# Expert results of 14 experts summed early by VectorE, those of the last two and of overflow added as one-hot products in PSUM

## The reference, cut to what matters

```python
# per token h: the two chosen experts eid and weights w of a router
gates = (one_hot(eid, 16) * w[..., None]).sum(1)
for e in range(16):
    y = (silu(h @ w_gate[e]) * (h @ w_up[e])) @ w_down[e]      # 1024 -> 512 -> 1024
    out = out + gates[:, e:e + 1] * y
xl = layer_norm(ALPHA * xl + g2_l * out, ln_ffn_g, ln_ffn_b)    # context tiles likewise in layer 0
```

## Time and profile before

| | |
|---|---|
| Time, three runs | 2450.93 us median (2446.91 to 2451.93) |
| The profiled execution | 2452.3 us; its span from the first to the last instruction is 2450.5 us |
| TensorE busy | 2274.0 us (93%), VectorE 1617.8 (66%), ScalarE 1329.9 (54%), GpSimd 242.4 (10%) |
| Mean granted TensorE clock | 0.978 of full speed |
| DMA | 575.35 MB, mean 235 GB/s |

### The profile page before, as it was taken

How to read it: one execution, slowest core, us unless ns; L and a number is a source line. 1 busy time by engine, 2 the same in 40 slices (tenths; PEclk the granted TensorE clock), 3 DMA queues, 4 the chain that set the end, 5 groups by cost and what they waited for, 6 DMA issues and landing times. The chain is left out here.

```text
span 2450.5 us, 29262 instructions
## 1 busy us (share of the span) xinstructions
PE 2274.0 (93%) x11460; PEld 1817.9 (74%) x11460; DVE 1617.8 (66%) x2358; ACT 1329.9 (54%) x2027; POOL 242.4 (10%) x214
## 2 busy tenths in 40 slices
PE   8999999999999999999989998999968997999994
PEld 7887767888788776888876576777756855788872
DVE  5556455655655645665555777899887467899983
ACT  5555544655555545455535614777753352688860
POOL 0001000000000100000003710011114000111101
PEclk9999999999999999999999998999989998999997
DMA  7765585576576567568631038999983334799994
GB/s 274 257 223 181 206 301 172 183 246 228 201 263 218 191 221 277 172 207 308 233 119 37 4 144 306 369 370 354 362 310 112 126 134 172 275 363 366 358 363 186
DMA packets 177731, 575.35 MB, mean 235 GB/s; under 512 B 20133, under 2 KB 28773, under 8 KB 145840
## 3 DMA queue, kind: packets, MB, share of 16 engines
q1 hardware_dynamic: 153120, 504.02, 58.0%
q10 hardware_dynamic: 13808, 51.06, 5.3%
q0 software_dynamic: 10656, 18.29, 2.2%
HBM read 538.69 MB, written 55.15 MB: 242 GB/s over the span
## 5 line engine op out<-in xcount | busy, mean ns | idle before, releaser
L325 DVE TENSOR_TENSOR LO<-RAW,HI 128x1024 fp32r<-128x1024 f32 x558 | 660.0, 1223 | 222.4 <-ACT HI L311 221.2
L311 ACT ACTIVATE HI<-RAW 128x1024 fp32r<-128x1024 f32 x558 | 571.3, 1056 | 371.0 <-PE PS L385 194.3
L383 PE MATMUL PS<-HI,FR 128*128 128x512 f32 (+1 forms) x1776 | 687.3, 387 | 13.6 <-DVE FR L458 7.5
L385 PE MATMUL PS<-HI,FR 128*128 128x512 f32 (+1 forms) x1776 | 680.3, 383 | 0.0
L384 PE MATMUL PS<-LO,FR 128*128 128x512 f32 (+1 forms) x1776 | 679.7, 383 | 0.0
L311 ACT ACTIVATE HI<-RAW,SM 128x512 fp32r<-128x512 f32 (+2 forms) x576 | 361.7, 684 | 276.3 <-PE PS L385 149.4
L327 DVE SCALAR_TENSOR_TENSOR LO<-RAW,SM,HI 128x512 fp32r<-128x512 f32 (+2 forms) x576 | 378.8, 710 | 172.7 <-ACT HI L311 172.5
L383 PEld LDWEIGHTS PS<-HI,FR 128*128 128x128 f32 x1776 | 335.5, 189 | 82.3 <-DVE FR L458 8.7
L385 PEld LDWEIGHTS PS<-HI,FR 128*128 128x128 f32 x1776 | 335.1, 189 | 65.9
L384 PEld LDWEIGHTS PS<-LO,FR 128*128 128x128 f32 x1776 | 335.3, 189 | 62.4
L458 DVE TENSOR_TENSOR FR<-PS,FR 128x512 fp32r<-128x512 f32 x224 | 143.9, 676 | 134.7 <-ACT FR L454 134.1
(11 more groups left out here) (346 smaller groups left out, 2334.6 us busy)
## 6 DMA issues: line engine op xcount, KB each, us to landing
RAW<-in_w_ffn_in SPq DMA_DIRECT2D x88, 1024.0 KB
RAW<-in_w_gate SPq DMA_DIRECT2D x68, 1024.0 KB, 8.5
RAW<-in_w_up SPq DMA_DIRECT2D x68, 1024.0 KB, 10.8
RAW<-in_w_down SPq DMA_DIRECT2D x64, 1024.0 KB
RAW<-in_w_ada SPq DMA_DIRECT2D x48, 1024.0 KB
RAW<-in_w_ffn_out SPq DMA_DIRECT2D x44, 1024.0 KB
RAW<-in_w_in SPq DMA_DIRECT2D x44, 1024.0 KB
YD<-CN ACTq DMA_DIRECT2D x32, 1024.0 KB, 5.4
```

Source lines behind the costliest of these rows:

```text
L311: e.activation(HI[:, i % NSPLIT, c], raw_of(j)[:, c], ACT.Copy, scale=1.0 if g is None else g).then_inc(*hi_done.up())
L325: e.tensor_tensor(LO[:, i % NSPLIT, c], raw_of(j)[:, c], hi, ALU.subtract).then_inc(*lo_done.up())
L383: e.matmul(o, h, hi[:, j, :], start=first and k + j == 0, stop=False)
L385: x = e.matmul(o, ll, hi[:, j, :], start=False, stop=end)
```

## The change

The stage's end is taken apart for the two image tiles. The context tiles keep their old way.

- **Early part.** `dve_late_weights` (expert 2) sets the weight and the slot of a result to zero where its expert is 14 or 15 or an overflow tile. `pool_take` gathers the two rows of each image token when experts 0 to 13 are in `YD`, ahead of `pool_further`. ScalarE scales, VectorE adds, multiplies with the gate and adds `ALPHA` times the stream, 1024 columns at a time, in `XL`.
- **Late part.** `dve_hot` (experts 3 to 6, three instructions of 128x128 each) builds a matrix that has a token's weight at the row that its result has in expert 14 or 15; TensorE transposes four of them in expert 7. The results of 14 and 15 are multiplied with the gate from `x_y` or PSUM (`dve_gate_late`), and `pe_add_late` multiplies them with the matrices into PSUM banks 4 to 7, one per tile and half. Overflow tiles add to the same banks (`more`, `dve_hot_more`) and no longer go through `YD` in layer 1. `dve_add_late` adds the bank to the stream and takes statistics.
- **Norms.** The steps of the attention stage's norm go from the stage's end into the experts: layer 0 one in each of experts 8 to 15, layer 1 one in each of 7 to 10. The six fold steps stand two by two in experts 4 to 6.
- **Tiles.** In layer 0 tile 0 is finished and its input for the attention made while tile 1 is added; the low parts of `qb p0` are placed between. In layer 0 the first two late products stand inside the down product of expert 15.
- **Loads.** Layer 1's last gain and bias (two rows of 4 KB spread over 128 partitions) are loaded after the last expert's weights instead of during the attention. The nine spins are gone.

The core of the diff (left out are the moved buffers, the exact form of `strips` and the counters):

```diff
+def pe_add_late(e, q, l, n, t, h, start, last):
+    q.wait_ge(*dve.at(f"m{l} gated {LATE[n]}{h}"))
+    return e.matmul(PS[4 + 2 * t + h][:, :], x_hot[:, 256 * n + P * t:256 * n + P * t + P],
+                    half_of(x_gated[l][n], h), start=start, stop=last)
...
+    def late(last):
+        if l == 0:
+            for t, h in each:
+                if t:
+                    if h == 0:
+                        for g in range(2):
+                            pe_free(q, 6 + g)
+                    pe_add_late(e, q, l, 0, t, h, True, False)
+                x = pe_add_late(e, q, l, 1, t, h, False, last)
+                if last:
+                    x.then_inc(pe.handle, 1)
+        else:
+            for t, h in each:
+                x = pe_add_late(e, q, l, 1, t, h, False, last)
+                if last:
+                    x.then_inc(pe.handle, 1)
+        return x
+    def more(i, last):
+        q.wait_ge(*more_dve.at(f"m{l} more {i} gated"))
+        for t, h in each:
+            if l == 0:
+                hot, y = x_hot_more[:, P * t:P * t + P], half_of(x_g[1], h)
+            else:
+                hot = x_hot[64 * h:64 * h + 64, 256 * (i % 2) + P * t:256 * (i % 2) + P * t + P]
+                y = x_y[0][64 * h:64 * h + 64, 0:512]
+            x = e.matmul(PS[4 + 2 * t + h][:, :], hot, y, start=False, stop=last)
...
+    def close(i):
+        if i == 0:
+            late(True)
+        elif l:
+            more(i - 1, True)
...
+        if i == 7:
+            q.wait_ge(*dve.at(f"{s} hot"))
+            b = pe_turn(e, q, f"{s} hot T", blocks(x_hot_T), rot)
+            freed[b] = [(act, f"{s} hot in")]
...
+            if i == NE - 1:
+                rot = Banks([0, 1, 2, 3])
...
+            def between():
+                if i == NE - 1:
+                    weighed_T(NE - 1)
+                elif i == NE and l == 0:
+                    q.wait_ge(*act.at(f"{s} hot in"))
+                    for h in range(2):
+                        pe_free(q, 4 + h)
+                        pe_add_late(e, q, l, 0, 0, h, True, False)
...
+    if l == 1:
+        q.wait_ge(*act.at(f"{s} hot in"))
+        for t in range(2):
+            for h in range(2):
+                pe_free(q, 4 + 2 * t + h)
+                pe_add_late(e, q, l, 0, t, h, True, False).then_inc(*pe.up(f"{s} late {t}{h}"))
     pe_further(e, q, l)
...
+        if i == 7:
+            q.wait_ge(*pe.at(f"{s} hot T"))
+            e.activation(x_hot, PS[bank[f"{s} hot T"]][:, :], ACT.Copy).then_inc(*act.up(f"{s} hot in"))
...
+            if i == NE:
+                for t in range(2):
+                    act_add_early(e, q, l, t)
+            for h in range(0 if l and i - 1 in LATE else 2):
                 q.wait_ge(*pe.at(f"{s} y {i - 1}{h} 0"))
+                if i == NE:
+                    q.wait_ge(*dve.at(f"{s} gated {i - 1}{h}"))
...
+            if l == 0 and i > NE - 2:
+                q.wait_ge(*act.at(f"{s} y in {i - 1}1"))
                 e.dma_start(YD[(i - 1) * P:i * P, :], y).then_inc(
...
+def act_add_early(e, q, l, t):
+    y = x_early[l][t][0]
+    q.wait_ge(*dve.at(f"m{l} early weights"))
+    q.wait_ge(*yf_in[t].at(f"m{l} y {t}"))
+    e.activation(y, y, ACT.Copy, scale=x_ew[:, t:t + 1]).then_inc(*act.up(f"m{l} first {t}"))
+def dve_sum_early(e, q, l, t):
+    ya, yb = x_early[l][t]
+    q.wait_ge(*act.at(f"m{l} first {t}"))
+    q.wait_ge(*yg_in[t].at(f"m{l} y {t}"))
+    e.scalar_tensor_tensor(ya, yb, x_ew[:, 2 + t:3 + t], ya, ALU.mult, ALU.add).then_inc(*dve.up(f"m{l} summed {t}"))
+def dve_gate_early(e, q, l, t):
...
+    for h in range(2):
+        q.wait_ge(*g2_in[0].at(f"{s} gate 0"))
+        if l:
+            q.wait_ge(*dve.at(f"{s} summed {n}"))
+        if l == 0 and n == 0:
+            q.wait_ge(*act.at(f"{s} y in {LATE[n]}{h}"))
+        else:
+            q.wait_ge(*pe.at(f"{s} y {LATE[n]}{h} 0"))
+        y = half_of(x_y[n], h) if l == 0 and n == 0 else PS[bank[f"{s} y {LATE[n]}{h}"]][:, :]
+        e.tensor_tensor(half_of(x_gated[l][n], h), y, half_of(HBS[0], h),
...
+def dve_add_late(e, q, l, t, h):
+    s, xs = f"m{l}", half_of(XL[:, t, :], h)
+    q.wait_ge(*pe.at(f"{s} sum {t}{h}"))
+    q.wait_ge(*dve.at(f"{s} z {t}"))
+    e.tensor_tensor(xs, xs, PS[4 + 2 * t + h][:, :], ALU.add).then_inc(*dve.up(f"{s} added {t}{h}"))
+    q.wait_ge(*dve.last())
+    e.bn_stats(stat[:, 16 * t + 6 * h:16 * t + 6 * h + 6], xs).then_inc(*dve.up())
...
 def pool_take(e, q, l, t):
     s, side = f"m{l}", slots(l)
     for k in range(2):
-        if t > 1:
-            q.wait_ge(*dve.at(f"{s} added {t - 2}1"))
-        e.indirect_dma_start(out=x_pair[t % 2][k], out_offset=None, in_=YD[0:X_TILES[l] * NE * P, :],
+        e.indirect_dma_start(out=(x_pair[t % 2] if t > 1 else x_early[l][t])[k], out_offset=None,
+                             in_=YD[0:(X_TILES[l] if t > 1 else 1) * NE * P, :],
                              in_offset=bass.IndirectOffsetOnAxis(ap=side[:, k, t:t + 1], axis=0)).then_inc(
                                  *(yg_in if k else yf_in)[t % 2].up(f"{s} y {t}", by=16))
...
+    e.tensor_scalar(early, col, NE - 2.5, None, ALU.is_lt).then_inc(*dve.up())
+    for n, late in enumerate(LATE):
+        e.tensor_scalar(by_result(x_lw[n]), col, float(late), None, ALU.is_equal).then_inc(*dve.up())
+    q.wait_ge(*dve.last())
+    e.tensor_tensor(slots(l)[:, :, 0:2], slot, early, ALU.mult).then_inc(*dve.up(f"{s} slots"))
+    for n in range(2):
+        e.tensor_tensor(by_result(x_lw[n]), by_result(x_lw[n]), ww, ALU.mult).then_inc(*dve.up())
+    e.tensor_tensor(early, early, ww, ALU.mult).then_inc(*dve.up(f"{s} early weights"))
...
+def dve_hot(e, q, l, n, t):
+    s, row = f"m{l}", by_result(x_gs[:, 0:8])
+    hot, share = x_hot_T[:, 256 * n + P * t:256 * n + P * t + P], by_result(x_lw[n])
+    q.wait_ge(*dve.last())
+    e.tensor_scalar(hot, C["iota"], row[:, 0, t:t + 1], share[:, 0, t:t + 1], ALU.is_equal, ALU.mult).then_inc(*dve.up())
+    e.tensor_scalar(x_hot_tmp, C["iota"], row[:, 1, t:t + 1], share[:, 1, t:t + 1], ALU.is_equal,
+                    ALU.mult).then_inc(*dve.up())
+    q.wait_ge(*dve.last())
+    e.tensor_tensor(hot, hot, x_hot_tmp, ALU.add).then_inc(*dve.up(f"{s} hot" if n and t else None))
...
+        if i == 2:
+            dve_late_weights(e, q, l)
+        if 3 <= i < 7:
+            dve_hot(e, q, l, (i - 3) // 2, (i - 3) % 2)
         if l == 0 and i == 4:
             q.wait_ge(*mod_out[0].at("mod 10"))
-        if l == 0 and 4 <= i < 10:
-            dve_fold_step(e, q, s, (i - 4) // 3, (i - 4) % 3, *x_fold[(i - 4) // 3], x_fold_t)
+        if l == 0 and 4 <= i < 7:
+            for k in (2 * i - 8, 2 * i - 7):
+                dve_fold_step(e, q, s, k // 3, k % 3, *x_fold[k // 3], x_fold_t)
+        if l == 0 and 8 <= i < NE:
+            dve_norm_step(e, q, "o0", "o0 again", (i - 8) // 2, i % 2)
+        if l == 1 and 7 <= i < 11:
+            dve_norm_step(e, q, "o1", "o1", (i - 7) // 2, (i - 7) % 2)
+        if l == 1 and i == 11:
+            dve_hot_more(e, q, l, 0, dve)
...
-    dve_norms(e, q, f"o{l}", ("o0 again", "o1")[l], O_TILES[l])
-    dve_further(e, q, l)
     if l == 0:
+        dve_gate_late(e, q, 0, 0)
+        dve_sum_early(e, q, 0, 0)
+        dve_gate_early(e, q, 0, 0)
+        dve_gate_late(e, q, 0, 1)
+        dve_add_early(e, q, 0, 0)
+        dve_further(e, q, 0)
+        for h in range(2):
+            dve_add_late(e, q, 0, 0, h)
+        dve_stats(e, q, s, 0)
+        dve_sum_early(e, q, 0, 1)
+        q.wait_ge(*pe.at("m0 sum 11"))
+        dve_modulate_b(e, q, 0)
+        dve_gate_early(e, q, 0, 1)
+        lo_parts(e, q, of["qb p0"][0], 1)
+        dve_hidden_lo(e, q, "qb", 0)
+        dve_add_early(e, q, 0, 1)
+        for h in range(2):
+            dve_add_late(e, q, 0, 1, h)
+        dve_stats(e, q, s, 1)
+        lo_parts(e, q, of["qb p0"][0], 1)
+        dve_modulate_b(e, q, 1)
         lo_parts(e, q, of["qb p0"][0])
-        dve_add_up(e, q, 0, 0)
-        dve_add_results(e, q, 0, 1)
-        dve_modulate_b(e, q, 0)
-        dve_add_gated(e, q, 0, 1, 0)
-        dve_hidden_lo(e, q, "qb", 0)
-        dve_add_gated(e, q, 0, 1, 1)
-        dve_stats(e, q, "m0", 1)
-        dve_modulate_b(e, q, 1)
         dve_hidden_lo(e, q, "qb", 1)
     else:
         for t in range(2):
-            dve_add_up(e, q, l, t)
-    if l == 1:
+            dve_sum_early(e, q, 1, t)
+            dve_gate_late(e, q, 1, t)
+        for t in range(2):
+            dve_gate_early(e, q, 1, t)
+            dve_add_early(e, q, 1, t)
+        dve_further(e, q, 1)
+        for t in range(2):
+            for h in range(2):
+                dve_add_late(e, q, 1, t, h)
+            dve_stats(e, q, s, t)
         dve_norms(e, q, s, s, (0, 1))
...
-    q.wait_ge(*more_yd.at(f"{s} all"))
+    for i in (12, 13):
+        q.wait_ge(*yd_out[i % 2].at(f"{s} y {i}"))
     q.wait_ge(*dve.at(f"{s} slots"))
+    if l == 0:
+        q.wait_ge(*pe.at("m0 xT 151"))
```

(25 more changed lines are left out.)

238 lines of the change are left out of this document (160 added, 78 removed).

## The result

The changed kernel takes 2469.91 us in the median (2463.75 to 2472.72, 9 runs), the kernel before 2450.93 us (9 runs). The ratio is 1.0070, 95% interval 1.0056 to 1.0083: slower by 17 to 19 us, where I had forecast 2444 us, faster, and a range up to 2458. Measured again it gave 1.0077 (1.0055 to 1.0099). The profiled execution took 2464.88 us, span 2462.8.

The account below looks back on a forecast made before the run. VectorE's order of work bounds layer 0's end; the experts run on three almost full resources, and the kernel's end leaves engines mostly idle. -8.9 + 3.5 + 3 - 4.4 = -6.8 us gave 2444 us, range 2434 to 2458.

Parts of the forecast that it names:

- Layer 0's experts: Late weights, matrices, paired fold steps and norm steps lengthen layer 0's experts by 3.5 us; from 0 to 15.
- Layer 0's end: From expert 15 into the next attention: 9.8 us earlier, less 0.9 for the early gathers, -8.9.
- my walk: VectorE's work at layer 0's end, priced step by step from 1809.4 to 1841.1, against 1850.9 before.
- Layer 1's experts: Late weights, matrices and norm steps lengthen layer 1's experts by 3 us; from 0 to 12.6.
- Layer 1's end: Kernel's end: -15.3 for the return, +3.4 for the start, +7.5 for the duration, -4.4; from -12 to +2.
- Return: After the last matmul, the round trip through `YD` is dropped: 13.8 us instead of 29.1, 15.3 less.
- Duration: The two overflow tiles take 8.1 us longer, for late and overflow products, transpose, gating and copies; rounded to 7.5.
- 3 are counted above: Of the overflow tiles' start coming 5 to 6 us later, 3 were taken as already counted; 3.4 booked.
- (b): VectorE becomes the bound inside experts 2 to 15: 27.6 us, ends return 8.9 and 6.9; +11.8, 2463; chance 0.15.
- (c): TensorE cold without spins, in tile 1's matmuls and the overflow tiles: half +5, 2449, all 2454; chance 0.12.
- Its two terms: Lower clock: at most 5 us on tile 1's 24 matmuls, up to 7 on eight float32 overflow products.
- (d): Early gathers land late in a full DMA, VectorE waits 5 us at layer 0's early sums: 2449; chance 0.08.

Follow-up runs that it names:

- three moved the start by 2.3 us at most: On the changed kernel with layer 0's norm steps an expert later, singly: expert 15 in free banks 1.0048; last gain/bias behind overflow weights 1.0048; early gates/adds in overflow tile 1.0034.
- with a fourth: Gate and up weights of the first overflow tile issued ahead of 2 MB of down weights, together with the three edits: 2455.23 us, 1.0027.

## Why the prediction was wrong, by its own steps

Means over all kernels with the same code in a stage (in brackets how many), less the mean of the three executions of before; kernels with like code lie up to 4.4 us on either side of their mean in a stage.

- **Layer 0's experts: +3.5 predicted, +15.2 measured. This is the step that failed.** "Experts 8 to 15 ask for 17.5 in about 18.8 us: covered, with 0.8 us together" counted VectorE's time and neither the loads that a norm step needs nor where SyncE issues them. The diff moves those loads from expert 12 (before, the line below), where they had some 58 us before their use (1750.9 to 1809.4), to expert 7, in front of a step in expert 8: 0.3 us.

```profile
1750.93 0.43 SPq L1382 DMA_DIRECT2D GB<-in_ln_attn_g  x1
```

  The parts: 296.5 with the wait (2) against 289.0 without it (7), so 7.5 for the wait; 289.0 against 284.4 without steps inside (2), so 4.6 for 10 us of norm steps, not 0.8; 2.2 for the folds in pairs (286.8 with them apart, 1), for which I had 2.7; 0.8 left for weights and matrices. The wait is shown: the medians without it are 0.2 to 0.35% nearer to the kernel before, 6 to 9 us. The smaller parts are estimates, as the two kernels without steps lie 4.9 us apart. The three with folds apart and four steps inside, at 284.3 to 284.8, fit them: 289.0 less 2.2 and half of 4.6 is 284.5.
- **Layer 0's end: -8.9 predicted.** By the end of the last addition of a context tile after expert 15's product it is 64.4 us (10) against 67.8, -3.4; by the whole stage 299.4 (10) against 304.0, -4.5. The first pair alone gave -9.0 and seemed to prove the step; it was the attention behind it, with the same code, that fell short in one execution. A late product took 0.9 us, as priced (3.60 for four at the kernel's end). But my walk had only the first two; the six behind the gating of expert 15, 5.4 us of TensorE (7.1 to 8.5 in seven executions of other kernels), stood in it at nothing. With them came TensorE's own order: 3.04 us without work before them, tile 0's last two parts ahead of tile 1's transposes, and those at 0.43 us a matmul. VectorE itself kept to my walk: in the changed kernel it ended the last two low parts at 1859.0, where the walk, begun at 1827.5, has 1857.9. The 4.75 us that it then stood for tile 1's transposes are most of what is missing. That the clock's part of this can be had back isn't shown.
- **Layer 1's experts: +3 predicted, 272.0 (13) against 265.8, +6.2.** Two executions without norm steps inside had 266.9 and 268.9, so I put some 4 us to them, their full price in a stretch where TensorE, VectorE and DMA are all full; the medians of the two kernels don't confirm it (0.9994 and 0.9995), and it stays open.
- **Layer 1's end: -4.4 predicted, 75.1 (7) against 77.1, -2.0 measured.** Return 15.1, predicted 15.3. Duration +4.5, predicted 7.5: four late products 3.7 (3.6), four overflow products 2.0 (2.7), and the matrix work is hidden. The start is 16.1 us behind the low parts against 8.0: +8.1, where I had 5 to 6 and booked 3.4, "3 are counted above". Nothing of it was counted above: that was the error, and 5 to 6 was too low besides. The last 0.5 lies before the last low part.
- **The rivals.** 2469.9 lies beyond (b), and (b) is not what happened: of its 27.6 us in the experts 21.4 were there, but 7.5 of them are one wait; and the ends gave back 6.5, not 15.8. (c) had TensorE's lower clock right (in 1848 to 1869 the granted clock is 0.76, before in the like stretch 0.92), but not its place: the matmuls of tile 1 follow every 0.23 us, and it is most of tile 0's that go at 0.43. Its two terms, 5 and 7 us, also add up to 12, where it said 10. (d) did not happen in layer 0; in layer 1 VectorE stood 2.84 us for gathered rows.
- **Sum.** 15.2 - 4.5 + 6.2 - 2.0 = +14.9 us, where the medians say 17 to 19. The 2 to 4 us between are not found. The two profiled executions of the changed kernel lie 5 us below its medians and the three of before 1.4 to 4.1 above theirs, so these five alone differ by 9.7 us; the sum is nearer because it takes in the other kernels.

The Trainium skill ("DMA: Bandwidth & Descriptors", Rules for kernel authors) says to issue a transfer early and wait for it late. The trace agrees at its price here: 10 us from issue to landing for 0.5 MB in a full stream, hidden when the issue stood 21 us ahead of the use.

## What to carry to other kernels

When a use is moved forward, look for every load that it needs and count from the issue, in its queue, to the new place of the use; an instruction that waits in front of the low parts stops the whole weight ring. Where an edit gives 0 to 2 us and the chain of waits names a new releaser each time, several chains of like length end there: try the edits together before giving one up (three moved the start by 2.3 us at most, with a fourth by 5 to 7). And one execution per kernel is not enough for terms of 4 us: cut all runs with the same code at the same instruction.

## What the runs showed of the hardware that I had not expected

- A row of 4 KB spread over 128 partitions (0.5 MB) took 9.9 and 10.6 us to land in a stream at 0.95 to 1.0 of the DMA engines (the DMA view of the changed kernel, 1660 to 1690):

```profile
GB<-in_ln_attn_g SPq DMA_DIRECT2D x1, 512.0 KB, 9.9
GB<-in_ln_attn_b SPq DMA_DIRECT2D x1, 512.0 KB, 10.6
```

- A plain float32 product of 128 rows and 512 columns takes 0.90 us, two matmul records of 0.59 us; one of 64 rows 0.50 us. In a stretch with a granted clock of 0.64, most of it at 1.2 GHz, six took 8.41 us, 1.40 each (the kernel with spins).
- A plain wait of VectorE for 10.4 us left TensorE without work so long that the granted clock fell to 0.55 and 0.50 in its last two slices; the next 12 matmuls followed every 0.43 us, and only from 1684.3 on every 0.23. In the sum of the layer's experts 7.5 us of the wait stayed.
